# Expert choice over 65 pair sums, and 32 activation tiles of the second layer kept in SBUF

## What is computed

```python
def peer(h, w_pq, sub_keys, u_tab, v_tab):
    q = (h @ w_pq).reshape(B, T, PEER_HEADS, 2, PEER_HALF)            # 8 heads
    s = jnp.einsum('bthcd,hckd->bthck', q, sub_keys)                 # 128 keys in each half
    top_s, top_i = lax.top_k(s, 16)
    cand = top_s[..., 0, :, None] + top_s[..., 1, None, :]           # 16 x 16 pair sums
    best_s, best_j = lax.top_k(cand.reshape(B, T, 8, 256), 16)
    i1 = jnp.take_along_axis(top_i[..., 0, :], best_j // 16, axis=-1)
    i2 = jnp.take_along_axis(top_i[..., 1, :], best_j % 16, axis=-1)
    expert = i1 * 128 + i2
    w = jax.nn.softmax(best_s, axis=-1)
    # for every token: sum over its 128 (head, choice) pairs of
    #   w * gelu(h . u_tab[expert]) * v_tab[expert]
```

## Time and profile before

| | |
|---|---|
| median of three runs | 3266.9 us |
| profiled execution: its time, its span | 3266.7 us, 3264.9 us |
| mean granted TensorE clock, as a share of 2.4 GHz | 0.956 |
| busy, share of the span | TensorE 93%, VectorE 76%, ScalarE 47%, GpSimd 29% |
| DMA | 830.7 MB, mean 254 GB/s |
| U phase, value phase of the first layer | about 395 to 1078, 1078 to 1600 us |
| U phase, value phase of the second layer | about 1865 to 2283, 2283 to 2602 us |

### The profile page before, as it was taken

The page is one execution under the profiler, slowest core; times in us unless marked ns, Lnnn a source line. Parts: engine busy times, 40 slices in busy tenths (PEclk is TensorE's granted clock), DMA queues, the critical chain, the costliest instruction groups (busy, mean ns, idle before and its releaser), DMA issues.

```text
span 3264.9 us, 49103 instructions
## 1 busy us (share of the span) xinstructions
PE 3020.8 (93%) x19164; PEld 2664.9 (82%) x19164; DVE 2491.9 (76%) x4940; ACT 1539.1 (47%) x2895; POOL 962.7 (29%) x883
## 2 busy tenths in 40 slices
PE   6998999989989999999879999898999999988898
PEld 4656799989989788888765899888998989755898
DVE  2696599897888688888758698997899865668653
ACT  3455435737557333333434547496555543232543
POOL 0000045555656344344000024455665300000000
PEclk9999999999999999999998999999999989977899
DMA  7384348968779999999437568899999967501444
GB/s 233 99 273 158 134 151 282 343 221 312 270 274 337 362 373 354 378 358 369 167 100 249 190 229 311 281 355 373 374 400 400 343 207 250 162 33 45 156 141 131
DMA packets 355495, 830.70 MB, mean 254 GB/s; under 512 B 21024, under 2 KB 217664, under 8 KB 335168
## 3 DMA queue, kind: packets, MB, share of 16 engines
q1 hardware_dynamic: 257216, 469.79, 41.4%
q0 software_dynamic: 95680, 353.46, 29.6%
q10 hardware_dynamic: 2368, 4.31, 0.4%
HBM read 750.90 MB, written 76.55 MB: 253 GB/s over the span
## 4 chain that ended last, share of the span: by engine, by line
PE 63%; DVE 24%; DMA 7%; ACT 4%; issue 2%; POOL 1%; DVEq 0%; SPq 0%; ACTq 0%; POOLq 0%
PE ps L1001 16%; PE ps L924 14%; PE ps L619 13%; DVE fr L1796 6%; DMA ring<-in_peer_v 4%; DVE area L1796 4%; DVE area L1804 4%; PE ps L980 3%; PE ps L1089 2%; PE ps L697 2%; PE ps L1081 2%; PE ps L853 1%; ACT fr L1245 1%; PE ps L636 1%; DVE acc L1796 1%
## 5 line engine op out<-in xcount | busy, mean ns | idle before, releaser
L1796 DVE TENSOR_TENSOR fr<-ring,fr 128x1024 fp32r<-128x1024 f32 x641 | 781.1, 1221 | 458.1 <-ACT fr L1245 443.1
L1245 ACT CAST fr<-ring 128x1024 fp32r<-128x1024 f32 x677 | 705.2, 1047 | 580.6 <-PE ps L1001 324.4
L924 PE MATMUL ps<-fr 128*128 128x384 f32 (+1 forms) x4784 | 852.2, 331 | 16.4 <-DVE fr L1796 16.4
L924 PEld LDWEIGHTS ps<-fr 128*128 128x128 f32 x4784 | 789.5, 192 | 22.6 <-DVE fr L1796 20.2
L1001 PE MATMUL ps<-fr 128*128 128x512 f32 x2304 | 525.3, 390 | 4.8 <-DVE fr L1796 4.8
L1001 PEld LDWEIGHTS ps<-fr 128*128 128x128 f32 x2304 | 434.5, 189 | 95.5 <-ACT area L1555 5.1
L619 PE MATMUL ps<-fr 128*128 128x256 f32 (+1 forms) x2928 | 416.9, 305 | 26.2 <-DVE fr L1796 26.2
L619 PEld LDWEIGHTS ps<-fr 128*128 128x128 f32 x2928 | 390.6, 194 | 52.3 <-DVE fr L1796 32.4
L2641 POOL DMA_INDIRECT plain<-in_peer_v,area x192 | 278.9, 1452 | 243.8 <-DVE area L1804 166.7
L2673 POOL DMA_DIRECT2D g_scratch<-area x256 | 145.1, 567 | 598.5 <-ACT area L1555 549.2
L1026 PE MATMUL ps<-fr 128*128 128x384 f32 x1024 | 301.9, 365 | 19.2 <-DVE fr L1796 18.4
(11 more groups left out here) (228 smaller groups left out, 4038.0 us busy)
## 6 DMA issues: line engine op xcount, KB each, us to landing
ring<-in_peer_uT SPq DMA_DIRECT2D x128, 1024.0 KB
ring<-in_peer_v SPq DMA_DIRECT2D x128, 1024.0 KB
ring<-in_w_mod SPq DMA_DIRECT2D x48, 1024.0 KB
w_scratch<-acc POOLq DMA_DIRECT2D x36, 1024.0 KB
g_scratch<-area POOLq DMA_DIRECT2D x128, 192.0 KB
area<-g_scratch POOLq DMA_DIRECT2D x64, 384.0 KB
area<-w_scratch POOLq DMA_DIRECT2D x16, 1536.0 KB
ring<-in_w_ada SPq DMA_DIRECT2D x24, 1024.0 KB
```

The costliest lines, as they stand in the source:

```text
L924: ins = e.matmul(o[:, 0:width], pairs[m][0], pairs[m][1], start=(m == 0), stop=(l == 0 and m == last), skip_group_check=l == 1)
L1245: e.copy(hi, x).then_inc(act.after(("high", name)), 1)
L1796: return e.tensor_tensor(o, a, b, op).then_inc(dve.after(*labels), 1)
```

## The change

**Choice.** The scores of both halves come sorted. A pair (i, j), counted from 0, can be among the best 16 only if (i+1)(j+1) is at most 16; the change forms 65 pair sums a head that hold all of these. `PAIRS` lists five rectangles of rows i: row 0 with 16 columns, rows 1-2 with 8, rows 3-6 with 4, rows 7-14 with 2, row 15 with 1. Five small sums for all eight heads at once take the place of the two sums of 128x1024, and `best16` runs over sets of 65 in place of 256. A winner's place no longer is 16i + j, so the decoding changes: `R1` becomes a float32 whose value is (i + 1 + a fraction)/128, made by an OR and a shift, and is compared by `is_ge` with the new constant `steps` (1/128 to 16/128); the "indices" it is multiplied with are the differences of neighbouring ones. The column is cut out by two more shifts.

**Kept tiles.** In the second layer (`KEPT = (0, 32)`) the GELU of tiles 96 to 127 is written to 32 tiles `b.kept` of 128x192 in SBUF: 26 lie over the query and feature buffers `b.qT` and `b.hX`, 6 behind `b.sum`, where the choice's buffers were (`b.cand` now takes 640 columns, not 1024). They are neither stored nor read back. The value phase walks tiles 96 to 127 first and 0 to 95 after (`v_order`), with the V tiles and the routing weights in the same order.

```diff
@@ Memory.peer
-        b.cand = lay.take(1024)
+        b.cand = lay.take(640)
...
+        if l == 1:
+            b.kept = [self.area[:, kept_at + i * D:kept_at + (i + 1) * D] for i in range(n)]
+            b.kept += [lay.take(D) for _ in range(KEPT[1] - n)]
...
+PAIRS = [((1 << r) - 1, min(1 << r, 17 - (1 << r)), 16 >> r) for r in range(5)]
+WIDTH = 65
+KEPT = (0, 32)
+def v_order(l, a):
+    return (a - KEPT[l]) % 128
...
+    def g_tile(self, l, a):
+        b = self.peers[l]
+        return b.kept[a] if a < KEPT[l] else b.GL[(a // 2) % 4][:, a % 2, :]
@@ scalar_program, gelu
-            if a >= b.ngs:
+            x = b.GS[a % b.ngs]
+            if a >= 128 - KEPT[l]:
+                x = b.kept[a + KEPT[l] - 128]
+                w.wait_ge(pe, ("rt", l, T // 128 - 1, 3))
+                w.wait_ge(pe, ("pu", l, max(PLAIN_TILES)))
+                if a >= 120:
+                    w.wait_ge(pe, ("ow", l, D // 4 - 1))
+            elif a >= b.ngs:
                 w.wait_ge(M.g_stored[a % b.ngs], ("g", l, a - b.ngs))
@@ vector_program, choose
-        for h0 in (0, 4):
-            cv = b.cand.rearrange("p (h a b) -> p h a b", h=4, a=16)
-            last()
-            tt(cv, tsv[:, h0:h0 + 4, 0, :].unsqueeze(3).to_broadcast([128, 4, 16, 16]),
-               tsv[:, h0:h0 + 4, 1, :].unsqueeze(2).to_broadcast([128, 4, 16, 16]), AD)
+        cv = b.cand.rearrange("p (h x) -> p h x", h=8)
+        for r, (i0, ni, nj) in enumerate(PAIRS):
+            tt(cv[:, :, 16 * r:16 * r + ni * nj].rearrange("p h (a b) -> p h a b", a=ni),
+               tsv[:, :, 0, i0:i0 + ni].unsqueeze(3).to_broadcast([128, 8, ni, nj]),
+               tsv[:, :, 1, 0:nj].unsqueeze(2).to_broadcast([128, 8, ni, nj]), AD)
+        last()
+        for h0 in (0, 4):
-            best16([(b.cand[:, 256 * j:256 * j + 256], b.SW[j], bs[:, h0 + j, :], bj[:, h0 + j, :]) for j in range(4)],
+            best16([(cv[:, h0 + j, 0:WIDTH], b.SW[j][:, 0:WIDTH], bs[:, h0 + j, :], bj[:, h0 + j, :]) for j in range(4)],
                    lambda i: fill(spread(fill_b, 5)[i], False))
...
-        ts(b.R1.bitcast(U32), b.BJ.bitcast(U32), 4, None, ALU.logical_shift_right, None)
-        ts(b.R2.bitcast(U32), b.BJ.bitcast(U32), 15, None, ALU.bitwise_and, None)
+        ts(b.R1.bitcast(U32), place, 1920, 19, ALU.bitwise_or, ALU.logical_shift_left)
+        ts(row, place, 4, None, ALU.logical_shift_right, None)
-        e.tensor_copy(b.R1f, b.R1.bitcast(U32)).then_inc(dve.after(), 1)
+        e.tensor_copy(ti_steps[:, :, 0], tiv[:, :, 0, 0]).then_inc(dve.after(), 1)
+        tt(ti_steps[:, :, 1:16], tiv[:, :, 0, 1:16], tiv[:, :, 0, 0:15], SU)
+        stt(low4, place, 15, row, ALU.bitwise_and, ALU.logical_shift_left)
+        stt(place, low4, 15, row, ALU.bitwise_and, ALU.logical_shift_right)
@@ vector_program, weigh
-            w.wait_ge(M.g_read[g % 4], ("g", l, g))
+            if a < KEPT[l]:
+                w.wait_ge(act, ("gelu", l, v_order(l, a)))
+            else:
+                w.wait_ge(M.g_read[g % 4], ("g", l, g))
@@ gpsimd_program
         def store_g(a):
+            if a >= 128 - KEPT[l]:
+                return
...
-            if g >= 4:
+            n = v_order(l, 2 * g)
+            if g >= KEPT[l] // 2 + 4:
                 w.wait_ge(dve, ("alow", l, 2 * g - 7))
...
-            if a % 2 == 1:
+            if a % 2 == 1 and a >= KEPT[l]:
                 load_g(a // 2 + 4)
```

More of the change, by code:

```diff
@@ L2142, in choose @@
+        last()
+        stt(place, low4, 15, row, ALU.bitwise_and, ALU.logical_shift_right)
+        last()
+        e.tensor_copy(b.R2f, place).then_inc(dve.after(), 1)
         ww = b.WW.rearrange("p (h r) -> p h r", r=16)
@@ L2146, in choose @@
         tt(ww, bs, b.mxs.unsqueeze(2).to_broadcast([128, 8, 16]), SU, ("wsub", l, t))
[L2147 removed]
+        i2_values = tiv[:, :, 1, :]
+        for Rf, marks, op, values, I in ((b.R1, "steps", ALU.is_ge, ti_steps, b.I1),
+                                         (b.R2f, "iota", ALU.is_equal, i2_values, b.I2)):
             part = spread(fill_c, 6)
@@ L2828, in constants @@
     put("iota", np.arange(128)[None, :])
+    put("steps", np.arange(1, 17)[None, :] / 128.0)
     put("eps", np.array([[1e-6, 1e-5]]))
```

44 lines of the change are left out of this document (22 added, 22 removed).

## The result

| | before | after |
|---|---|---|
| median of the runs | 3269.95 us (3266.49 to 3274.32, 4 runs) | 3241.47 us (3235.98 to 3244.59, 4 runs) |
| after / before | | 0.991, 95% interval 0.9888 to 0.9933 |
| profiled execution: time, span | 3266.7, 3264.9 us | 3238.5, 3236.4 us |

The change wins 28.5 us of span, and 3211 us had been forecast, with a range from 3199 to 3234. About half of the forecast gain came.

What follows compares the result with a forecast made beforehand. TensorE, 93% busy, was taken as the bound, so time comes from its waits and from DMA- or VectorE-paced stretches: choice 37, U phase 8, value phase 11, 56 us off 3266.7, forecast 3211 us, range 3199 to 3234.

Steps and rivals of the forecast that it cites:

- The small operations: Choice: pair sums with best16 fall from 17.5 us by 9.2; decoding's small operations grow by 1.0 on 0.96 us.
- VectorE ends each block's choice 8.2 us earlier: Each block's choice: 9.2 us saved in the pair sums less 1.0 us more decoding; range 3.3 to 9.2 us.
- VectorE can't run ahead at will ... so I count 7.5 us: First layer's third block: low halves need ScalarE's high halves and freed buffers, so 7.5 of 8.2 us count.
- I cost it at nothing, and at up to 2 us in the range: Choice: VectorE operations delayed by GpSimd's low halves; the five sums meet at most one, priced 0, up to 2 us.
- The waits: Ends of five blocks' choices: TensorE's waits for VectorE and low halves shrink, 31.1 us in sum.
- The clock's 6 us: After the choice's waits TensorE's clock no longer falls: 1.2 us for each of five blocks.
- Rival D: Choice: VectorE's idle time moves to waits for ScalarE's high halves, TensorE stays as late; near 3262 us, chance 0.03.
- Rival C: First layer's pair sums and decoding: GpSimd holds up every small operation; slower, 3278 us at worst, chance 0.03.
- Rival B: Choice: operations narrower than 128 columns don't get cheaper; 3232 us, or 3240 with GpSimd on top, chance 0.12.
- The U phase's end: Second layer: GELUs no longer wait for stores, the DMAs are late next; 8 us won, range 0 to 10.
- The value phase: Second layer: VectorE's stand of 8.1 us and 3.1 MB of reads go at 400 GB/s; 11 us, range 8 to 13.
- Rival A: U and value phases: DMAs take back what the kept tiles free, only the choice pays; 3230 us, chance 0.13.

Runs made afterwards that it cites:

- the old filling: TensorE's filling steps left as in the kernel before; moving 6 and 12 a block from pair sums to decoding in the changed kernel gave 3240.5 us.
- the two repeats: The changed kernel itself, unedited, run again on two other chips: medians 3243.3 and 3241.9 us.
- alone: The kept tiles without the new choice, which stays as in the kernel before: 3252.2 us.
- rows_even: Changed kernel with the second layer's 64 gathered U rows spread over the whole second block instead of the tiles behind its pair sums: 3240.1 us.
- half_decode: Changed kernel with the decoding's marks, values and products as bfloat16 and constants 64 bytes a partition longer: 3222.2 us.
- half_again: Changed kernel with the bfloat16 decoding and the 64 bytes longer constants, run once more on another chip: 3223.1 us.
- vector_lows: Changed kernel with VectorE in place of GpSimd making the first layer's low halves beside the pair sums: 3244.2 us.

## Why the prediction was wrong

- **The small operations** were right: the sets of 65 took 0.21 to 0.23 us an operation (0.2 to 0.23 forecast), the pair sums 8.0 us (8.3). The decoding's small rows went from 0.96 to 1.7 us in the second layer (2058.37 to 2060.09); in the second block of the first layer they took 3.9 us, as one cast met a low half of GpSimd's and took 2.35.
- **"VectorE ends each block's choice 8.2 us earlier"** is the step that failed. VectorE did save 8.7 us a block, and the prediction carried them to the end of `choose` as if next to nothing lay between. Counted from the last search product, `choose` ended 2.9, 4.3 and 3.1 us earlier in the first layer's second to fourth block, and not at all in the second layer (0.9 and 0.2 us later). Two terms were mis-sized:
  - "VectorE can't run ahead at will ... so I count 7.5 us" names the mechanism and prices it at 0.7 us a block. VectorE's waits for ScalarE's high halves took 3.7, 0 and 1.3 us in the first layer, and all of it in the second. There TensorE was the slower engine up to the decoding, 50.00 of 50 us busy, a row that could be read in the trace of before; VectorE stood 8.5 to 9.8 us for high halves ahead of the decoding in each block, 0 to 0.6 before.
  - GpSimd's low halves, "I cost it at nothing, and at up to 2 us in the range", because the five sums meet at most one. It wasn't the sums that met them: the pair sums became shorter, so the decoding begins while GpSimd still makes low halves (third block: the decoding's first row at 698.52 us and GpSimd's last low half over at 697.50 before, 686.83 and 695.54 after), and a cast and operations of 128x1024 took 2.1, 4.3 and 4.4 us more than usual in the three blocks. In the second and fourth a wait for a high half came behind them anyway; in the third they are all that was lost.
- **The waits** of the earlier trace rows were taken as what VectorE's lateness costs. The wait at line 624 is the decoding's, behind the last low half that TensorE needs before it: one value, to 0.6 us, for two lengths of the pair sums, in every block compared but the first layer's second with the old filling. The waits that answered to the pair sums are those for low halves within the decoding (5.3 and 4.0 us). Choice: 37 us forecast, 10.7 measured. The clock's 6 us hung on the waits and mostly stayed out with them.
- **Rival D** ("VectorE's idle time moves to waits for ScalarE's high halves and TensorE stays as late") is what happened in the second layer, and in part in the first. It got a chance of 0.03 for the reason that "at line 624 it is the end of `choose` itself that TensorE waits for", which is true and no argument: the wait for it can be as long as before. **Rival C** named the neighbour that took half of what VectorE saved in the first layer's third block, but priced it on the small operations, where it would have made the kernel slower.
- **Rival B's** time (3232) is near the result for another reason: narrow operations do get cheaper.
- **The U phase's end**: 8 us forecast, within 0 to 10; 3.0 in the first profile, 3.3 and 4.7 in the two repeats, 5.4 alone. The step "what is late next are the DMAs" had the right neighbour, the gathered rows, but gave it no price. In rows_even, with fewer rows there, the stage is 8.3 us shorter than before; since rows are work too and no run moves them without the kept tiles, that doesn't show that the kept tiles' 8 us are to be had.
- **The value phase**: 11 forecast, 10.6 measured, 11.1 alone, at the rate the text took. Rival A falls for this phase. I set the row's flat 400 GB/s against a rule of the Trainium skill ("SBUF — State Buffer", the DMA setup-cost knee: an asymptote of 436) and called the row the limit. It is one of this placement: 64 bytes further on the same queues moved 411 to 419. VectorE was busy for 145 of 150 us there, 138 at the old place, so little is left below it.
- **The range**: "not all at one end" it says, but 3200 to 3226 is what the three parts give with all at one end (67 and 40 us off).

## What to carry to other kernels

Before a saving on one engine is carried to the end of a stage, find the next thing that this engine waits for and look who is at 100% up to there; where two engines go hand in hand through shared buffers, each stretch between two meetings has its own bound, and only the bound's time counts. A wait at the end of a stage tells the length of its last stretch, so shorten that one first: 0.53 us off each of 24 multiplications in the decoding (13 us of VectorE) won 10 us of the median, about as much as 9.5 us off the pair sums of each of six blocks. A shorter stretch also moves what follows it in time: here the decoding began beside another engine's work that it had missed before, which the trace of before can show for the new time. And where two DMA-bound kernels differ in memory layout, a control with the layout alone belongs beside them.

## What was not expected of the hardware

- Moving the ring and the area behind it by 64 bytes raised the queues' rate from 2400 to 2550 us, in the middle of the value phase, from 398 to 400 GB/s to 411 (unused constants) and 416 (half_decode); half_again, the same code as half_decode on another chip, moved 419 to 420 from 2350 to 2500 us.
- Beside a low half of GpSimd's, a subtraction or multiplication of 128x1024 on VectorE took 3.1 to 3.5 us in place of 1.22, and a cast of 128 columns 2.35 in place of 0.23. In the first layer the 16 multiplications lost 4.2 us to this. Where VectorE stood for a high half soon after (second and fourth block) the collision most likely only shortened that wait; where it didn't (third block) some 2.8 of 4.3 us reached TensorE, by the estimate at vector_lows.
- MAX8, MATCH_REPLACE8 and FIND_INDEX8 fall with the width down to 65 columns: 0.21 to 0.22 us on average, from 0.28 to 0.29 at 128 and 0.41 to 0.42 at 256.
